# A linear-attention layer rebuilt around one 128-token chunk per tile of tokens

## The reference, cut to what matters

```
proj = rms_norm(h) @ w_in                    # 1024 -> 3*1024 (q,k,v) + 1024 (z) + 16
qkv  = silu(causal_depthwise_conv(proj[qkv]))   # 4 taps
q, k = l2_norm(q), l2_norm(k);  beta = sigmoid(b);  g = -exp(a_log) * softplus(a + dt)
# per head (8 heads of 128), per chunk of C tokens:
a    = tril((beta*k) @ k.T * decay, -1) + I
u, w = solve(a, beta*v), solve(a, beta*k*exp(g))
v_new = u - w @ S;   o = (q*exp(g)) @ S + (tril(q @ k.T) * decay) @ v_new
S    = S * exp(g_last) + (k*exp(g_last-g)).T @ v_new
h    = h + (rms_norm(o) * silu(z)) @ w_out
```

## Time and profile before

| what | value |
|---|---|
| median of 3 runs | 1740.83 us (1733.78 to 1742.19) |
| span of the profiled execution, first to last instruction | 1740.3 us |
| its own time | not given apart from the span |
| share of the span: PE, DVE, ACT, POOL busy | 95%, 69%, 52%, 2% |
| mean granted TensorE clock | 0.961 |
| first dense matmul (end of the part that is changed) | 315.19 us |

### The profile page before, as it was taken

How to read it: one execution, slowest core, us unless ns; L and a number is a source line. 1 busy time by engine, 2 the same in 40 slices (tenths; PEclk the granted TensorE clock), 3 DMA queues, 4 the chain that set the end, 5 groups by cost and what they waited for, 6 DMA issues and landing times.

```text
span 1740.3 us, 20929 instructions
## 1 busy us (share of the span) xinstructions
PE 1645.9 (95%) x8292; PEld 1363.9 (78%) x8292; DVE 1198.3 (69%) x1195; ACT 901.3 (52%) x831; POOL 28.1 (2%) x29
## 2 busy tenths in 40 slices
PE   7997998899998969799999999999999999999998
PEld 6886974899997456588888888888888788888886
DVE  3648424544444063388888798798898898898885
ACT  1222421334432143176667666676667667676664
POOL 0001001000000010000000000000000000000000
PEclk9999999999999976799999999999999999999999
DMA  9400006545555410299999899899899899999991
GB/s 354 168 1 10 1 1 242 195 175 174 186 192 195 144 49 16 81 334 368 341 356 375 309 376 374 310 373 377 308 375 373 311 375 349 336 373 341 346 373 42
DMA packets 183534, 434.04 MB, mean 249 GB/s; under 512 B 5181, under 2 KB 5333, under 8 KB 183472
## 3 DMA queue, kind: packets, MB, share of 16 engines
q1 hardware_dynamic: 182528, 430.57, 68.0%
q0 software_dynamic: 944, 2.60, 0.5%
HBM read 432.08 MB, written 1.07 MB: 249 GB/s over the span
## 4 chain that ended last, share of the span: by engine, by line
PE 84%; DVE 8%; issue 6%; ACT 1%; POOL 1%; DMA 0%; SPq 0%; POOLq 0%; DVEq 0%; ACTq 0%
PE bank L889 12%; PE bank L891 12%; PE bank L890 12%; PE bank L515 6%; PE bank L874 5%; PE bank L876 5%; PE bank L875 5%; PE bank L694 3%; PE bank L696 3%; PE bank L695 3%; PE bank L475 2%; DVE ring_r L1532 2%; PE bank L826 2%; PE bank L656 2%; PE bank L716 2%
## 5 line engine op out<-in xcount | busy, mean ns | idle before, releaser
L1532 DVE TENSOR_TENSOR ring_r<-ring,buf_r 128x2048 fp32r<-128x2048 f32 x336 | 750.5, 2284 | 44.0 <-ACT buf_r L1093 44.0
L1093 ACT ACTIVATE buf_r<-ring 128x2048 fp32r<-128x2048 f32 x336 | 627.6, 1913 | 62.2 <-PE bank L876 62.2
L889 PE MATMUL bank<-ring_r,buf_r 128*128 128x512 f32 x896 | 354.2, 395 | 1.6 <-DVE buf_r L1615 1.6
L891 PE MATMUL bank<-buf_r,buf_r 128*128 128x512 f32 x896 | 349.6, 390 | 0.0
L890 PE MATMUL bank<-buf_r,buf_r 128*128 128x512 f32 x896 | 348.9, 389 | 0.0
L891 PEld LDWEIGHTS bank<-buf_r,buf_r 128*128 128x128 f32 x896 | 168.2, 188 | 35.9
L889 PEld LDWEIGHTS bank<-ring_r,buf_r 128*128 128x128 f32 x896 | 168.3, 188 | 34.9 <-DVE buf_r L1615 1.7
L890 PEld LDWEIGHTS bank<-buf_r,buf_r 128*128 128x128 f32 x896 | 168.4, 188 | 33.6
L874 PE MATMUL bank<-ring_r,buf_r 128*128 128x512 f32 x448 | 176.5, 394 | 8.0 <-DVE buf_r L1628 7.9
L876 PE MATMUL bank<-buf_r,buf_r 128*128 128x512 f32 x448 | 174.6, 390 | 0.0
L875 PE MATMUL bank<-buf_r,buf_r 128*128 128x512 f32 x448 | 174.4, 389 | 0.0
(11 more groups left out here) (240 smaller groups left out, 1751.8 us busy)
## 6 DMA issues: line engine op xcount, KB each, us to landing
ring<-in_moe_w_gate SPq DMA_DIRECT2D x56, 2048.0 KB, 8.0
ring<-in_moe_w_up SPq DMA_DIRECT2D x56, 2048.0 KB, 8.1
ring<-in_moe_w_down SPq DMA_DIRECT2D x56, 2048.0 KB, 8.0
ring<-in_a_w_in SPq DMA_DIRECT2D x8, 2048.0 KB, 16.5
ring<-in_dense_w_gate SPq DMA_DIRECT2D x7, 2048.0 KB, 8.6
ring<-in_dense_w_up SPq DMA_DIRECT2D x7, 2048.0 KB, 7.8
ring<-in_dense_w_down SPq DMA_DIRECT2D x7, 2048.0 KB, 7.9
ring<-in_a_w_out SPq DMA_DIRECT2D x2, 2048.0 KB, 8.0
```

Of the source, the lines that this page charges most:

```text
L889: pe.matmul(o, xh, low[:, c], start=k == 0, stop=False)
L891: ins = pe.matmul(o, xh, high[:, c], start=False, stop=k == KT - 1)
L1093: act.activation(HB[m % NHB], half_words(m, U_MOE), ACT.Copy).then_inc(m_wh, 1)
L1532: dve.tensor_tensor(half_low(m, U_MOE), half_words(m, U_MOE), HB[m % NHB], ALU.subtract).then_inc(m_wl, 1)
```

## The change

Nothing after the linear attention changes but the slot that a weight unit lies in.

- **Chunks of 128 tokens.** `CH` is gone, the masks cover 128 tokens, `NLEV` is 7 (levels 1 to 6 on TensorE), and the recurrence has two chunks: chunk 0 needs one state product (`ks_mm`), chunk 1 reads the state, and no state is written after it.
- **Norms as row factors.** k isn't normed: the Gram matrix of raw k is multiplied by decay times beta/|k|^2 of the row; the decay matrix is scaled in place and masked later (`mask`). The three scaled copies of k, the back transposes of q, k, beta*k and the token copies of q are gone. Values are scaled by |k| (`values`, a power of 1/2 on POOL). The squares of q are summed by 16 matmuls with one column (`"s"`, `qn_mm`) and enter the output's norm as an addend.
- **After the solve** TensorE runs `yv_mm`, `w_mm` and `ks_mm` (8 products of 128 columns each), project(13), the 8 products of chunk 0's output, 16 products `vn_mm`, project(14), 4 + 4 transposes, project(15), 16 products for chunk 1's output, and the output projection.
- **Order of projections.** `IN_COLS` makes it k, v, q, z. Ahead of the solve stand project(0), the gates, project(1), the cumulated decays, project(2), the eight of 512 columns, project(3), and what the diff shows. TensorE issues projections 0 to 6 ahead of the solve, `project(6 + lv)` after Z of each level (7 to 12), and 13, 14, 15 between the products of the recurrence. They go to banks 6 and 7 in turn (`FILLS`, `fill_free`), together with the value transposes, the products q k and the sums of q squared; the solve's Z has only banks 4 and 5.
- **Ring.** Units 0 to 9 use three slots (`FRONT` = 3: unit n waits for unit n - 3); the dense units take the slots in the order `RING` and start as soon as the array in a slot is dead, the first at `proj_mm` 16. The mask levels are loaded by POOL at the start, into `R[7]`.
- **Output projection** by token tile: tile 0 while the norm of tile 1 is under way.

```diff
-CH = 64
+IN_COLS = [2, 3, 4, 5, 0, 1, 6, 7]
+FRONT = 3
+RING = [1, 5, 4, 3, 6, 2, 0]
+FILLS = ([("p", f) for f in range(4, 10)] + [("v", 0), ("v", 1), ("p", 10), ("v", 2), ("v", 3), ("p", 11), ("a", 0),
+         ("a", 1), ("p", 12), ("a", 2), ("a", 3), ("s", 0), ("p", 13), ("p", 14), ("p", 15)])
+def fill_bank(kind, n):
+    return 6 + FILLS.index((kind, n)) % 2
...
+                if FRONT <= n < U_FF:
+                    sp.wait_ge(*released(n - FRONT))
+                elif i == 0:
+                    sp.wait_ge(proj_mm, 16)
+                elif i == 1:
+                    sp.wait_ge(ks_mm, 2)
+                elif i == 2:
+                    sp.wait_ge(vn_mm, 2)
+                elif i in (3, 4):
+                    sp.wait_ge(o_mm, 4)
+                elif i in (5, 6):
+                    sp.wait_ge(wo_mm, 4)
...
+            def fill_free(kind, n):
+                k = FILLS.index((kind, n))
...
+                was, f = FILLS[k - 2]
+                if was == "p" and f < N_Z:
+                    pe.wait_ge(conv_done, f + 1)
+                elif was == "p":
+                    pe.wait_ge(z_done, f - N_Z + 1)
+                elif was == "v":
+                    pe.wait_ge(vt_ready, f + 1)
+                elif was == "a":
+                    pe.wait_ge(attn_ready, f + 1)
...
+            project(3)
+            for g in range(2):
+                key_tokens(g)
+            for g in range(2):
+                gram(g)
+            project(4)
+            for g in range(2, 4):
+                key_tokens(g)
+            for g in range(2, 4):
+                gram(g)
+            project(5)
+            project(6)
...
                 for g in range(4):
                     pe.wait_ge(y_ready, 4 * (lv - 1) + g + 1)
+                    if g >= 2:
+                        pe.wait_ge(u_ready, 4 * lv + g - 1)
...
+                project(6 + lv)
+                if lv in (3, 4):
+                    for g in (2 * lv - 6, 2 * lv - 5):
+                        value_tokens(g)
+                if lv >= 5:
+                    for g in (2 * lv - 10, 2 * lv - 9):
+                        attn(g)
                 if lv < NLEV - 1:
                     turn(lv)
...
+            project(13)
+            pe.wait_ge(attn_ready, 4)
...
+            project(14)
...
+            pe.wait_ge(vn_ready, 2)
+            out_tp(0)
+            project(15)
...
+            w_out(0, 0, range(KT))
+            w_out(0, 1, range(4))
+            out_tp(1)
+            w_out(0, 1, range(4, KT))
...
+            solve_in(0)
+            conv(4)
+            solve_in(1)
+            conv(5)
+            level(1)
+            conv(6)
+            conv(7)
+            level(2)
+            conv(8)
+            level(3)
+            conv(9)
+            dve.wait_ge(pow_out, powers[0])
+            for g in range(2):
+                values(g)
+            mask(0)
+            mask(1)
+            level(4)
+            conv(10)
+            for g in range(2, 4):
+                values(g)
+            mask(2)
+            mask(3)
+            level(5)
+            conv(11)
+            for g in range(2):
+                attn(g)
...
+            level(6)
+            for g in range(2, 4):
+                attn(g)
```

More of the change, by code:

```diff
@@ L93, in constants @@
         "neg_half": np.full((P, 32), -0.5),
+        "half": np.full((P, UN), 0.5),
         "iota8": np.tile(np.arange(EXPERTS), (P, 1)),
@@ new lines, in gram @@
+            def gram(g):
+                half, t = g // 2, g % 2
+                if g < 2:
+                    pe.wait_ge(dt_ready, g + 1)
+                    if g == 1:
+                        pe.wait_ge(egb_ready, 1)
+                else:
+                    pe.wait_ge(m_ready, g - 1)
+                for i in range(4):
+                    kk = CONV[:, HEADS + 4 * half + i, tok(t)]
+                    m = pe.matmul(quad(4 + g % 2, i), kk, kk, start=True, stop=True)
+                m.then_inc(gram_mm, 1)
@@ new lines, in _ @@
+                    for i in range(4):
+                        u = 4 * g + i
+                        m = pe.matmul(quad(4 + g % 2, i), X[3][:, u, :], R[3][:, u, :], start=True, stop=True)
+                    m.then_inc(z_mm, 1)
+                project(6 + lv)
[5 more added lines that the diff above has]
+                        attn(g)
@@ new lines, in _ @@
+            m.then_inc(qn_mm, 1)
+            pe.wait_ge(u_ready, 4 * NLEV)
+            for half in range(2):
+                for u in range(8 * half, 8 * half + 4):
+                    m = pe.matmul(quad(2 * half, u % 4), R[3][:, u, :], R[2][:, u, :], start=True, stop=True)
+                m.then_inc(yv_mm, 1)
+            pe.wait_ge(tok_v, 2)
+            for half in range(2):
+                for u in range(8 * half + 4, 8 * half + 8):
+                    m = pe.matmul(quad(4 + half, u % 4), R[5][:, u, :], R[3][:, u, :], start=True, stop=True)
+                m.then_inc(w_mm, 1)
@@ new lines, in _ @@
+            pe.wait_ge(t0_scaled, 1)
+            for half in range(2):
+                pe.wait_ge(yv_ready, half + 1)
+                for u in range(8 * half, 8 * half + 4):
+                    m = pe.matmul(quad(1 + 2 * half, u % 4), R[5][:, u, :], HSU[:, u, :], start=True, stop=True)
+                m.then_inc(ks_mm, 1)
+            project(13)
+            pe.wait_ge(attn_ready, 4)
+            for half in range(2):
+                for u in range(8 * half, 8 * half + 4):
+                    m = pe.matmul(quad(2 * half, u % 4), R[0][:, u, :], HSU[:, u, :], start=True, stop=True)
+                m.then_inc(o_mm, 1)
@@ new lines, in _ @@
+            for half in range(2):
+                pe.wait_ge(w_ready, half + 1)
+                pe.wait_ge(st_ready, half + 1)
+                for i in range(4):
+                    u = 8 * half + 4 + i
+                    pe.matmul(quad(4 + half, i), R[3][:, u, :], R[2][:, u, :], start=True, stop=False)
+                    m = pe.matmul(quad(4 + half, i), R[6][:, 8 * half + i, :], STATE[:, 4 * half + i, :],
+                                  start=False, stop=True)
+                m.then_inc(vn_mm, 1)
@@ L1024, in dense_high @@
+            z_out(14)
+            z_out(15)
+            for half in range(2):
+                act.wait_ge(o_mm, 2 + half + 1)
+                act.activation(X[3][:, quads(2 * half + 1), :], as_quad(1 + 2 * half), ACT.Square).then_inc(o_sq, 1)
             def dense_high(m):
```

663 lines of the change are left out of this document (325 added, 338 removed).

## The result

The changed kernel takes 1694.78 us (median of four runs, 1694.43 to 1697.52) against 1737.57 us for the kernel before, measured beside it (1733.78 to 1742.19): 42.8 us less, ratio 0.9769, 95% interval 0.9738 to 0.9800. Forecast were 1704 us, 37.1 us less, and a range from 1690 to 1720.

The account below looks back on a forecast made before the run. Bound by TensorE, with projections, preparation and solve leaving one engine waiting in turn. 16.3 start + 231.4 work + 1.0 Z banks + 8.9 bank waits + 10.0 clock = 267.6 us against 304.7, so 1740.8 - 37.1 = 1703.7; range 1690 to 1720.

Parts of the forecast that it names:

- the column sums: Behind the solve: 16 one-column products summing q squared on TensorE, put at 4.6 us, bounds 3.6 and 9.2.
- The three bank waits: After project(9), (10), (11): the pair's second fill waits for the convolution freeing its bank, 3.1, 3.1, 2.7 us, 8.9 together.
- The clock: In the edited part: four falls of TensorE's granted clock at 2.5 us each, 10.0 us, bounds 2.5 and 20.
- The distance of levels: In the solve: Y, Z, a projection and a turn take 15.8 us per level, 19 with a bank wait.
- The front: Ahead of the solve: TensorE reaches turn(0) without a wait, VectorE's slack there being 1.6 to 3 us.
- The total: Whole kernel: 37.1 us less, 1703.7 us, with dense layer, attention and experts running from their start as now.
- The first: Linear attention part: the walked queues with two to six low-clock episodes, 1693 to 1714 us; chance 0.66.
- The second (low clock at every level): Solve and behind: clock falls at every level and again afterwards, 10 to 22 us more, 1714 to 1726; chance 0.12.
- The third (VectorE's queue): Ahead of and in the solve: VectorE's queue sets the pace, 20 us more, 1724, or 1729; chance 0.11.
- The fourth (loads exposed): Weight loads: the three-slot ring exposes five loads by 8 us each, 40 us, 1744, nothing gained; chance 0.02.
- The fifth (low clock without end): Solve: low clock never ends, about 100 us of TensorE work takes 200, time 1794 us, slower; chance 0.03.
- The sixth (no bank wait, hardly an episode): Edited part: no low-clock episode but the first and no bank wait, 1693 us and less, to 1687; chance 0.06.

Follow-up runs that it names:

- the shifted one: Changed kernel plus two more passes of squares on VectorE ahead of all else: median 1698.26 us of four, 1697.20 without one of 3581.22; ratio 0.9771.
- the kernel with the fills moved: Changed kernel, second value quad of levels 3 and 4 and second q k quad of level 5 issued after the next level's Y: 1674.9 us, ratio 0.966.

## Why the prediction was right

**The sum.** Forecast end of the last output product 267.6 us, measured 267.67; first dense matmul about 278, measured 278.33. That it fits to 0.1 us is luck: term by term it is less exact and errors cancel, and traces with the same code or nearly so put the first dense matmul at 273.5 (wide column sums), 280.3 (extra work between the levels) and 277.9 with TensorE starting 2.1 us later (the shifted one).
- The gates' 16-column products took 3.49 us (I had 4.59, a row that was in part at half clock, and had priced that episode again under the clock), the column sums 3.59 at the full clock, in the kernel with the fills moved (I had 4.6 from the same row; the lower bound of 3.6 was it). 2.1 too much.
- Z loses 0.52 us to its two banks in levels 1 to 3 (4.09 from Z to the projection against 3.57), 0.6 in 4 and 5 and 0.2 in 6, 3.0 in all, not 1.0: besides the fourth quad, which waits for VectorE's second subtraction as I had it, the third waits for the first subtraction. 2.0 too little.
- The three bank waits: 3.25, 3.25, 2.80, sum 9.3; forecast 3.1, 3.1, 2.7.
- The clock: 10.0 forecast for four episodes. Levels 3, 4 and 5 lost 6.8 to it and the column sums 3.2, 10.0 in all; but the episode at the start, which I had counted, wasn't there, and the third wait, which I hadn't, had one. Of the eight experiments on the changed kernel seven had the start's episode (1.6 to 2.2 us; only the one with extra work in front hadn't), and the five that keep the three waits had one or three episodes behind these. The number was right, but its places were luck.
- The distance of levels: 16.3 us without a wait, forecast 15.8; but 21.7, 23.5 and 23.5 with one, where I had given 19. There I had left out the two extra quads of each (0.9 or 1.8 us) and the low clock, though the sum has both.

**The front.** No wait ahead of turn(0), as walked. The last quad of solve_in(1) was done 2.4 us before turn(0), forecast 2. The tightest link was one that I hadn't walked, the bank of the fourth Gram quad, free 1.5 us before it was wanted; the extra work in front came out there, 6.4 of its 9.13 us as wait.

**The total.** 42.8 against 37.1 us: the edited part gave 36.9 in the profile. The rest I had counted at nothing, "run from their start as now". That holds for the instructions and not for the clock at which they run: the attention section was 7.7 us shorter in the changed kernel's trace, 0.80 of the clock for 0.75. It is no gain of the change that could be shown, since the kernel before spreads as much by itself: against its two shorter executions beside the changed kernel (1733.78 and 1734.32) the change took off 39.3 us, against its two longer ones (1740.83 and 1742.19) 46.7, and 42.8 lies between because the median of four falls between the groups. With both kernels shifted, where no execution of the kernel before was of the longer group, it is 37.4. So 37 to 39 us is what the runs give to the change. The absolute time, 1704, was 9 us too high: it starts from 1740.8, an execution of the longer group, as the profile is. The clock of the attention section was no term of my sum, and the range held what it did only since other bounds were wide.

**The rivals.** The first, the forecast: four episodes where it allowed two to six. The second (low clock at every level): out, three of six levels at most, always those with a bank wait. The third (VectorE's queue): not in this kernel, but real; 9.13 us in front cost 10.6 at turn(0), 4.2 of them low clock. The fourth (loads exposed): out, by a ring of two. The fifth (low clock without end): every episode within the solve was over in under 8 us. The sixth (no bank wait, hardly an episode): not in this kernel, but it is what the moved fills made of it. Of two-source operations the Trainium skill ("VectorE: DVE Perf Modes", the perf-mode tier table) lets one expect twice the time of one-source ones; the quads ran at 0.60 us as in the earlier trace rows, VectorE was busy for 29.37 of 61 us in levels 3 to 5, and the row was right to decide. What I had not seen is that the waits which the interleaving brings, though I had them in the sum, cost more than it gives: 0.1 us a level against 15.7 us of waits and low clock.

**What stays open:** what decides which waits are followed by the low clock. In the six traces with the three bank waits the first was followed by it each time, the second and third in two of them (the changed kernel and the one with extra work between the levels). Also open: why the episode at the column sums comes and goes with these waits, and what puts an execution of the kernel before into its longer group. The stretch behind the first dense matmul came out 12.0 and 3.5 us different in two shifted kernels and the same in the third; with one trace each this doesn't show that the shift did it.

## What to carry to other kernels

Where an engine is handed work between the steps of a chain, look at which buffer each piece must wait for: two pieces behind one another in two alternating banks make the second wait for the consumer of what was issued just before. Move such a piece one step later before counting the cover as gained; here that was worth 18 us in the trace and 20 in the median (15 and 13 in the shifted pair), and made the fastest kernel of the study (1674.9 us). And read the granted clock of sections that you haven't touched before you credit an edit with their time, and look at the single executions of the kernel that you start from: where they fall into two groups, a forecast from one of them or a median between them is off by their distance.

## What the runs showed of the hardware that was not expected

- The same code over the same data ran for 385.4 to 400.2 us in twelve traces, with a granted clock of 0.75 to 0.87 in its attention section; 31 executions of the kernel before fall into two groups, 1730.19 to 1735.05 and 1738.73 to 1745.04 us.
- 2.5 us of work at the start cost 2.4 us in the changed kernel, 2.8 in the kernel before (beside its shorter group), and 9.1 with the fills moved.
- Clock episodes are no function of the wait alone: 3.25 us waits in identical places were followed by full clock or by 1.2 GHz, and a wait of 2.80 us was followed by 1.2 GHz in the changed kernel and by full clock in four other traces.
- 32 instructions (16 fp32 products) with 16 moving columns last 3.49 us at the full clock, with one column 3.59, and with 128 columns 3.57: up to 128 columns the count of them made no difference here. Each of these products has weights of its own; that this is the reason isn't shown.
